# Two column groups of the modulation between the projection groups, and branch C's projections between the attention units

## The reference

```python
h = rms_norm(x) * (1 + scale_m) + shift_m        # adaLN: six rows of 1024 per sequence, from silu(c) @ w_ada + b_ada
z = h @ w_in                                     # 1024 -> u (512) | qB, kB, vB (768 each) | qC 512 | kC 128 | vC 128 | gates 3072
# A: pooling of u. B: three groups of dilated attention, 4 heads each, merged by their softmax denominators.
# C: window-128 attention, 8 query heads on 2 key heads, with sinks. B and C add a T5 bias table.
y = (g_a * a + g_b * (b @ w_b_up) + g_c * (c @ w_c_up)) @ w_out
x = x + gate_m * rms_norm(y)
h = rms_norm(x) * (1 + scale_f) + shift_f
x = x + gate_f * rms_norm(moe(h))                # 64 experts, top 8, and one shared expert
```

## Time and profile before

| | |
|---|---|
| three runs | 1744.22, 1748.67, 1750.66 us (median 1748.67) |
| profiled execution | 1733.79 us, its span 1732.1 us |
| TensorE busy, mean granted clock | 90% of the span, 0.928 |
| VectorE, ScalarE, GpSimd busy | 27%, 29%, 15% |
| DMA | 461.29 MB, 266 GB/s mean |
| first projection matmul starts | 110.03 us |
| first attention matmul starts | 353.94 us |
| last attention output is emptied | 473.9 us |

### The profile page before, as it was taken

The page is one execution under the profiler, slowest core; times in us unless marked ns, Lnnn a source line. Parts: engine busy times, 40 slices in busy tenths (PEclk is TensorE's granted clock), DMA queues, the critical chain, the costliest instruction groups (busy, mean ns, idle before and its releaser), DMA issues.

```text
span 1732.1 us, 22957 instructions
## 1 busy us (share of the span) xinstructions
PE 1563.6 (90%) x7181; PEld 881.1 (51%) x7182; DVE 474.7 (27%) x953; ACT 509.6 (29%) x854; POOL 264.9 (15%) x322
## 2 busy tenths in 40 slices
PE   4489999989897999997889879999999999999955
PEld 1057888877764777775345423333333333333311
DVE  2030000145672111111266422222222222212137
ACT  2110000045641000000233234444454444444321
POOL 0030051000300000000111112212122221211153
PEclk7689999966997999998989989999999999999988
DMA  8892379472388936549534299999879998999867
GB/s 289 302 337 26 50 235 331 163 241 64 131 279 257 302 94 203 178 160 329 207 123 169 85 364 393 345 383 411 325 275 342 405 420 341 420 417 422 321 266 249
DMA packets 140516, 461.29 MB, mean 266 GB/s; under 512 B 13401, under 2 KB 78425, under 8 KB 111308
## 3 DMA queue, kind: packets, MB, share of 16 engines
q1 hardware_dynamic: 117853, 331.36, 52.3%
q0 software_dynamic: 22608, 129.18, 21.1%
HBM read 424.80 MB, written 109.28 MB: 308 GB/s over the span
## 4 chain that ended last, share of the span: by engine, by line
PE 79%; DMA 7%; DVE 3%; SPq 3%; POOL 2%; issue 2%; ACT 2%; another core or an unknown queue 1%; ACTq 0%; POOLq 0%; DVEq 0%
PE bank L2107 72%; PE bank L2639 3%; POOL arena L1166 2%; DMA arena<-in_we_down 2%; SPq L783 1%; PE bank L2272 1%; DMA arena<-in_cache_b 1%; PE bank L2661 1%; PE bank L2313 1%; DMA arena<-in_w_in 1%; DMA arena<-in_w_ada 1%; DMA mods<-arena 1%; DMA arena<-in_we_gate 1%; DMA pscale<-in_pool_scale 1%
## 5 line engine op out<-in xcount | busy, mean ns | idle before, releaser
L2107 PE MATMUL bank<-arena 128*64 (+10 forms) x6096 | 1417.0, 513 | 118.4 <-DMA arena<-in_w_ada 26.5
L2107 PEld LDWEIGHTS bank<-arena 128*64 128x64 f32 (+3 forms) x6096 | 748.7, 173 | 680.9 <-issue 467.3
L1184 ACT ACTIVATE arena<-bank 128x512 f32<-128x512 f32 (+6 forms) x152 | 75.1, 505 | 350.5 <-PE bank L2107 219.8
L2026 DVE COPY arena<-bank 128x512 f32<-128x512 f32 x52 | 36.0, 692 | 409.0 <-PE bank L2639 409.0
L1441 ACT ACTIVATE arena<-arena 128x2048 f32 x52 | 99.7, 1918 | 19.5 <-DMA arena<-in_we_gate 15.7
L1128 POOL DMA_INDIRECT arena<-h2rows,icol x54 | 95.6, 1771 | 46.6 <-POOL icol L1124 46.6
L1450 ACT ACTIVATE arena<-arena 128x2048 f32 x52 | 99.3, 1910 | 11.4 <-issue 11.4
L1533 DVE COPY arena<-bank 128x512 f32<-128x512 f32 (+6 forms) x70 | 41.8, 606 | 209.7 <-PE bank L2107 185.8
L1460 ACT ACTIVATE arena<-bank 128x256 f32<-128x256 f32 x52 | 19.9, 383 | 239.5 <-PE bank L2107 239.5
L1323 ACT ACTIVATE arena<-bank 128x288 f32<-128x288 f32 x48 | 19.7, 410 | 233.6 <-PE bank L2107 233.6
L1085 POOL DMA_DIRECT2D out<-in_cache_b x24 | 12.0, 507 | 429.5 <-PE bank L2107 429.5
(11 more groups left out here) (235 smaller groups left out, 732.3 us busy)
## 6 DMA issues: line engine op xcount, KB each, us to landing
arena<-in_we_gate SPq DMA_DIRECT2D x64, 1024.0 KB, 11.2
arena<-in_we_up SPq DMA_DIRECT2D x64, 1024.0 KB, 13.6
arena<-in_we_down SPq DMA_DIRECT2D x64, 1024.0 KB, 11.0
out<-in_cache_b POOLq DMA_DIRECT2D x8, 4080.0 KB, 15.0
yrows<-arena POOLq DMA_DIRECT2D x52, 512.0 KB, 9.2
arena<-in_w_ada SPq DMA_DIRECT2D x12, 2048.0 KB, 16.7
arena<-in_cache_b SPq DMA_DIRECT2D x18, 1024.0 KB, 8.4
arena<-in_w_in SPq DMA_DIRECT2D x7, 2048.0 KB, 15.5
```

Source lines behind the costliest of these rows:

```text
L1184: act.activation(out, pick(bank), ACT.Copy).then_inc(emptied["A"], 1)
L2026: dve.tensor_copy(xT[:, 512:1024], psb[2][:, :]).then_inc(xt_dve, 1)
L2107: return pe.matmul(out, lhsT, rhs, start=first, stop=last)
```

## The change

Modulation group 0 alone stays at the start. Groups 1 and 2 are computed between projection groups, in bank 7, which is taken out of the ring there. The small loads, the first write of `mods` and the read of `modb` move from SyncE to ScalarE's queue. Sinks and `pscale` get a semaphore of their own (`sinks_in`). Silu is one activation. Scale by the norm and by `modb` is one VectorE instruction, and ScalarE's L1212 is gone. The `ada` loads 4 to 11 and the `in` loads interleave, in slots 2, 3 and 0, 1. SyncE waits for the first transposed tile before the state load and the `toep` writes; the third `in` load and `ada` loads 6 to 11 come behind these. Branch C's 13 keys (104 matmuls) go between the attention units, 5 matmuls for each step from step 0 on, in banks 6 and 7; the ring has banks 0 to 5 there. C's key transposes come at step 22. `stage` moves to slot 3, so the first load into that slot waits for the merged output of B, and the `kv_out` wait moves to C's first output.

```diff
@@ plan()
-    fill(("ada", 1), "D")
+    ring["set"], ring["n"] = list(range(7)), 0
...
+        if c == 3:
+            fill(("ada", 1), "D", 7)
...
+    fill(("ada", 2), "D", 7)
...
-    for c in range(6, 10):
-        for h in range(2):
-            fill(("q", c, h), "AD"[h])
-    for t in range(TILES):
-        fill(("kvc", t), "AD"[t % 2])
...
+    ring["set"], ring["n"] = list(range(6)), 0
+    def between(s, place):
+        for x in beside(s, place):
+            if x % KD == KD - 1:
+                j = x // KD
+                fill(BESIDE[j], "AD"[j % 2], 6 + j % 2)
...
+BESIDE = [("q", c, h) for c in range(6, 10) for h in range(2)] + [("kvc", t) for t in range(TILES)]
+KEYS_AT = 22
+def beside(s, place):
+    lo, hi = ((0, 2), (2, 4), (4, 5))[place]
+    return range(5 * s + lo, min(5 * s + hi, KD * len(BESIDE)))
@@ loads()
-    out = [(("ada", g), g % 4) for g in range(12)]
-    out += [(("in", g), g % 4) for g in range(7)]
+    out = [(("ada", g), g) for g in range(4)] + [(("ada", g), 2 + g % 2) for g in range(4, 12)]
+    out += [(("in", g), g % 2 if g < 6 else 2) for g in range(7)]
@@
-        stage = at(A_KTM, 3, PT_ * 264)
+        stage = at(3 * SLOT, 3, PT_ * 264)
@@ ScalarE
-            act.activation(crow[0:9, D:2 * D], crow[0:9, 0:D], ACT.Exp, scale=-1.0).then_inc(c_exp, 1)
+            act.activation(crow[0:9, D:2 * D], crow[0:9, 0:D], ACT.Silu).then_inc(c_silu, 1)
...
+            act.wait_ge(mods_rows, 1)
+            for j in range(4):
+                act.dma_start(mods[:, j // 2, 512 * (j % 2):512 * (j % 2) + 512], ada[32 * j:32 * j + 9, 0, :]
+                              ).then_inc(mods_out, 16)
+            act.wait_ge(mods_out, 16 * 4)
@@ VectorE
-            dve.wait_ge(gains_in, 16 * 8)
-            link(dve.tensor_scalar(sinkb[:], sinkb[:], -1.0, None, ALU.mult))
+            dve.wait_ge(gains_in, 16 * 4)
...
-                dve.tensor_tensor(hbuf[0:r, t % 2, :], hbuf[0:r, t % 2, :], modb[0:r, s, :],
-                                  ALU.mult).then_inc(hA_ready, 1)
+                dve.scalar_tensor_tensor(hbuf[0:r, t % 2, :], xall[0:r, t, :], stat[0:r, 0, t:t + 1], modb[0:r, s, :],
+                                         ALU.mult, ALU.mult).then_inc(hA_ready, 1)
@@ TensorE
             for c in range(4):
                 by_channel(("u", c), w, c * P)
+            ada_piece(1, 0)
+            ada_piece(1, 1)
             w = wait_load(pe, ("in", 1))
             for c in range(4):
                 by_channel(("q", c), w, c * P)
+            ada_piece(1, 2)
+            ada_piece(1, 3)
...
+                    ada_piece(2, 0)
+                    ada_piece(2, 1)
...
+            ada_piece(2, 2)
+            ada_piece(2, 3)
```

More of the change, by code:

```diff
@@ L809, in spread @@
                     sp.dma_start(to[0:NS, 2 * n + 1, :], sample_rows(q)).then_inc(done, 16)
-            spread(modb, (1, 0), modb_in)
-            for g in range(7, 12):
-                load(("ada", g))
+            load(("in", 0))
+            load(("in", 1))
+            load(("ada", 4))
+            load(("ada", 5))
+            sp.wait_ge(fills_done, INDEX[("hT", 0, 1)] + 1)
             sp.dma_start(staterow[0:NB * PSTATE, :], state_pool[0].rearrange("b t c -> (b t) c")).then_inc(state_in, 16)
-            for g in range(4):
-                load(("in", g))
             wait_emptied(sp, ("gtab", 2))
@@ L825, in _ @@
                              stab[h0:h1, n * NT * NK:(n + 1) * NT * NK]).then_inc(tables_out, 16)
+            load(("in", 2))
+            load(("ada", 6))
+            load(("ada", 7))
+            load(("in", 3))
+            load(("ada", 8))
+            load(("ada", 9))
+            load(("in", 4))
+            load(("ada", 10))
+            load(("ada", 11))
             sp.wait_ge(mods_rows, 2)
@@ L829, in _ @@
                              ).then_inc(mods_out, 16)
-            for g in range(4, 7):
+            for g in range(5, 7):
                 load(("in", g))
@@ L872, in _ @@
             kload = [k for k, _ in LOADS if k[0] == "K"]
-            for key in kload[:4]:
+            for key in kload[1:3]:
                 load(key)
@@ L1250, in _ @@
             act.wait_ge(tables_out, 16 * 8)
-            for m in range(0, 7, 2):
+            for m in range(0, 6, 2):
                 empty(("kT", m), kT[:, m, 0:SEQ])
@@ L1256, in _ @@
             for s in range(len(UNITS) + LAGO):
+                if s == KEYS_AT:
+                    empty(("kT", 6), kT[:, 6, 0:SEQ])
+                between(s, 0)
                 u = s - LAGT
@@ L1276, in _ @@
                     ins.then_inc(probs_ready, 1)
+                between(s, 2)
                 if s - LAGO == COMBINE_AT:
@@ L1712, in _ @@
                     outputs(s - LAGO)
+                between(s, 2)
+                if 0 <= s - LAGO < len(UNITS):
                     if s - LAGO == COMBINE_AT:
@@ L2153, in _ @@
                 close(mm(bank[0:20, 0:w], relT[0:BINS, :], oh_smp[0:BINS, 480 * n:480 * n + w], True, True))
-            for kk in range(4):
-                ada_piece(1, kk)
             for t in range(TILES):
@@ L2208, in _, with between @@
                     by_token(("v", g, t), w, (0, 256, 0)[g], t, g > 0)
-            for c in range(6, 8):
-                by_channel(("q", c), w, 256 + (c - 6) * P)
-            w = wait_load(pe, ("in", 6))
-            for c in range(8, 10):
-                by_channel(("q", c), w, (c - 8) * P)
-            for t in range(TILES):
-                by_token(("kvc", t), w, 256, t, False)
+            def between(s, place):
+                for x in beside(s, place):
+                    j, k = divmod(x, KD)
+                    key = BESIDE[j]
+                    if k == 0:
+                        bank_for(pe, key)
+                    bank = psb[6 + j % 2]
+                    w = wait_load(pe, ("in", 5 if j < 4 else 6))
+                    if key[0] == "q":
+                        col = 256 + (key[1] - 6) * P if j < 4 else (key[1] - 8) * P
+                        ins = mm(bank[:, 0:288], w[:, 512 * k + col:512 * k + col + P],
+                                 hT[:, k, 288 * key[2]:288 * key[2] + 288], k == 0, k == KD - 1)
+                    else:
+                        ins = mm(bank[0:parts(key[1]), 0:256], hT[:, k, toks(key[1])],
+                                 w[:, 512 * k + 256:512 * k + 512], k == 0, k == KD - 1)
+                    if k == KD - 1:
+                        close(ins)
             bank = bank_for(pe, ("uout", 0))
@@ L2228, in _, with turned_own_keys @@
                     wait_emptied(pe, ("k", g, t))
-                wait_emptied(pe, ("kvc", t))
-            for m in range(7):
+            def turned_own_keys(m):
                 bank = bank_for(pe, ("kT", m))
@@ L2234, in _ @@
                 close(ins)
[L2235 to L2241 removed]
+            for m in range(6):
+                turned_own_keys(m)
+            for m in range(6):
                 wait_emptied(pe, ("kT", m))
@@ L2275, in _ @@
                     close(ins)
+                between(s, 1)
                 u = s - LAGO
```

216 lines of the change are left out of this document (118 added, 98 removed).

## The result

The changed kernel takes **1791.4 us** (median of four runs, 1789.7 to 1801.1) where the kernel before takes 1748.7 (1744.2 to 1750.7): ratio 1.026, 95% interval 1.0225 to 1.0295. It is slower by 43 us; forecast were 1761 and a range up to 1784.

What follows compares the result with a forecast made beforehand. Bound by DMA at the start, TensorE in the projections and TensorE at half clock in early attention. -19 + 15.4 + 46 - 49.7 + 18.9 = +11.6 made the profiled execution 1746, the median 1761 us; range 1712 to 1784.

Steps and rivals of the forecast that it cites:

- Wait for `ada` 6: In the projections TensorE waits for this load, held behind the toep and sbias writes in SyncE's queue: +46 us.
- the table writes hold back little: Rival at TensorE's wait for `ada` 6: the 46 us vanish and the kernel gets faster, 1715 us; chance 16%.
- (a): Start: VectorE no longer waits for sinks and `pscale`; rows of `mods` there at 52 us in place of 54.03.
- (b): Start: write of `mods` takes 4 us instead of 12.44; after its read `modb` is there at 72.5, before 86.54.
- so I double 6.5 to about 12.5: Start: read of `modb`, 6.5 us of engine time, doubled to about 12.5 because it runs beside SyncE's loads.
- (c): Start: the hT stage, from `modb` to the first projection, takes 18.5 us where it took 23.5.
- The third rival: Start: small transfers starve beside 2 MB loads, rows at 56 and a write of 12.44; +12, 1773 us; chance 7%.
- Modulation pieces +15.4: Projections: eight pieces move from a stage where TensorE waited to one where it never waits, 1.92 us each.
- C's projections -49.7: Projection stage: C's projections leave it, -48.6 us, and with them 1.1 us of C's key transposes.
- half of 2.69 is 1.35: Attention: steps of 2.69 us at 1.2 GHz halve at 2.4 GHz; with C's matmuls a step is 3.8 us.
- 1 for `u_out`: Attention: ScalarE's wait for `u_out` while the cache copies run costs 1 us, part of the stage's +18.9.
- Later stages shift as a whole: Behind the attention, from 474 us on, the code is the same and its time changes by 0.

Runs made afterwards that it cites:

- tables_spread: Changed kernel with the toep writes spread between loads in SyncE's queue and sbias behind `ada` 11; 1746.8 us, ratio 1.000 to the kernel before.
- sbias_later: Changed kernel with the four sbias writes moved from ahead of the third `in` load to behind `ada` 11; 1792.8 us, ratio 1.025 to the kernel before.
- Gain_first: Changed kernel where VectorE waits only for the first gain load before the first modulation rows, for the other three later; 1798.3 us (one run).
- front_clear: all_three with SyncE issuing the second `in` load and `ada` 4 and 5 only after the read of `modb` has landed; 1725.2 us, ratio 0.990.
- uout_early: Changed kernel with the two `u_out` transposes and their output moved from the projections' end to behind the last modulation piece; 1777.5 us (one run).
- front_block: front_clear with C's projections in one block behind the first attention step's scores instead of five matmuls per step; 1740.4 us, ratio 0.997.
- all_three: Changed kernel with the edits of tables_spread, uout_early and gain_first together; 1733.1 us, ratio 0.992 to the kernel before.
- all_group1: all_three with the second group's four modulation pieces back in the stage of the tiles, `ada` 6 and 7 loaded there; 1724.6 us, ratio 0.987.

## Why the prediction was wrong

The side was right, the size was not: 43 us slower, against 12, and outside the range. By its steps:

- **Wait for `ada` 6: right, for a partly wrong reason.** 46 forecast, of it 44 and 1.6 as waits; 47.8 and 1.3 measured, and tables_spread shows that it is the loss. But it was built from two terms, 77.57 for `toep` and 34.70 for `sbias`. sbias_later shows that it is `toep`'s data nearly throughout, at 28 GB/s and a share of 0.23 for the four-head writes and 51 GB/s and 0.45 for the eight-head one. The sum was right since it was measured as a whole. The rival "the table writes hold back little" is refuted.
- **Start, (a) and (b): the failed step "I take 52" and "so I double 6.5 to about 12.5".** Rows at 58.5, `modb` at 82.1. I priced each transfer by itself, and for the write wrote that little stood before it in its queue. Gain_first shows otherwise: made 10.6 us earlier, the rows gave nothing. The write waited for the small loads ahead of it in ScalarE's queue, and the read ran beside the loads of SyncE's; front_clear, which takes 6 MB of those out of the way, gains 12 us at the read. The term was -7.9, 11 us short of -19: 6.5 for the rows, 2.2 for the write, 0.9 for the read and 1.5 for (c), which was 20 us. The range of -35 to -8 ends where it came out; added up again from the ends of (a) and (b), 73 and 103 us, it is -37 to -7. The third rival, with 7%, had about this size (+12), but by rows at 56 and a write of 12.44; here the rows were the larger part, and the write took 6.1.
- **The skill's two rules on (b).** The write took 6.08 us, so it didn't keep its 12.44. In gain_first it took 11.65, with a DMA share of 0.83 from 48 to 56 us and 1.01 behind it, and landed 0.8 us behind the last small load of its own queue. A second queue spared the write SyncE's backlog in order, not that of its own queue. Of the page "DMA: Bandwidth & Descriptors" of the Trainium skill, the section "Queues, rings and completion order" (engines take turns between queues) fits both numbers. By "Issuing engines are not separate DMA queues", which leaves a second issuing engine only the issue time, the first should have stayed near 12.44; that all queues share the engines, as it also says, fits the read, which ended 20.4 us behind the write beside SyncE's loads (gain_first) and 8.7 without them (front_clear). My error was to treat the choice between the two as the whole question.
- **Modulation pieces +15.4, C's projections -49.7:** together with the wait +11.7, measured +17.1. All in all held; the two waits, 47.8 and 1.3 us where I had 44 and 1.6, account for 3.5 of the difference, the rest I did not separate.
- **Attention: the failed step "half of 2.69 is 1.35", and "1 for `u_out`".** The clock did rise, which was the bold part. But the step did not halve with it: from T(0) to T(1) it was 1.81 us at 0.50 and 1.46 at 1.00, the next one 2.05 with the clock at full for the first half (front_block), and the mixed step 4.42 and not 3.8. Without the wait for `u_out` the attention takes 150.0 us (uout_early) against the forecast 139, and these steps are most of the 11 us. It could be suspected beforehand: the only step seen at full clock, in the earlier trace rows, was 1.90, and I halved the slow one instead. `u_out` cost 10 us where I had 1: I named the wait and the cache copies beside it, and didn't price a small write by what landed beside such copies. Moving C gave 17 us (front_block against front_clear, in the attention; 13 to 15 in the whole) where I had 31, below the bound of 20.
- **Later stages shift as a whole:** nearly. 8.8 us instead of 0; the lower clock at the first matmuls behind the attention has 3 of them, the rest has no cause here.
- **Median and profile:** the sum stood on an execution 15 us below its median, and I moved the result up by that. The execution of the changed kernel was at its median, so the terms miss by 46 us and the median only by 30. That the second number is the smaller is luck, in which execution of the kernel before was profiled.

The change as such was not the mistake: all_three keeps all of it, moves table writes, `u_out` and a wait, and is 0.8% faster than the kernel before; front_clear and all_group1 are 1.0 and 1.3% faster.

## What to carry to other kernels

When a transfer is moved behind others in a queue, price it by the time until the data ahead has drained (bytes over the rate seen for writes of that shape), not by how long the issues last, and look for stretches where that queue waits for a slot anyway: small and slow writes belong there. On a chain of transfers one late link is no gain by itself; ask what stands ahead of its successors in their own queue and what else moves beside them. When a clock is expected to rise, take the step from rows at that clock, form by form: a step of short matmuls of changing form went from 1.81 us to 1.46, not to half.

## What the hardware showed that I had not expected

- The issue of the same `in` load lasts 2.3 us, or 28.5 us behind `toep`; that of the same `sbias` writes 38.8 us behind `toep` or 1.4 us behind 2 MB loads. That an issue is held until the slow writes ahead leave room fits all four numbers.
- Writes of four source rows run at a DMA share of 0.23 and 28 GB/s when SyncE issues them, one of eight rows at 0.45 and 51 GB/s; when GpSimd issues the same writes it is 0.97 and 101 GB/s.
- A score matmul on 64 rows takes 474 ns on average at the lower clock and 419 ns at the higher, and four of them between matmuls of other forms 1.29 and 1.20 us; twelve in a row took 2.10 us at the higher.
- The early write of `mods` in ScalarE's queue landed 0.7 to 0.9 us behind the last small load ahead of it in that queue in all five runs that have it early, once at a DMA share of only 0.10. Why that load of 2.5 KB itself lands 17 us or more after its issue (40.2 to 57.3 in front_clear) is open.
